# Twelve weight rests per hybrid attention loop: from VectorE's queue to GpSimd's

## The reference, cut to what matters

```python
def hybrid_mixer(h, w_in, b_in, w_out, sinks, group_gain, rel_bias):
    proj = h @ w_in + b_in
    qa, ka, va, qb, kb, vb = jnp.split(proj, IN_SPLITS, axis=-1)
    ...
    ya = swa_attention(qa, ka, va, sinks, rel_bias[:, :SWA_Q_HEADS])   # 8 heads, window of 128, a sink
    yb = moba_attention(qb, kb, vb, rel_bias[:, SWA_Q_HEADS:])         # 8 heads, causal on 256 tokens
    y = jnp.concatenate([rmsnorm(ya, group_gain[:SWA_WIDTH]),
                         rmsnorm(yb, group_gain[SWA_WIDTH:])], axis=-1)
    return y @ w_out
```

## Time and profile before

| | |
|---|---|
| median of 3 runs | 3169.53 us (3164.65 to 3184.48) |
| the profiled execution | 3166.69 us |
| its span in the trace | 3164.9 us |
| TensorE busy in the span | 97% |
| VectorE busy | 72% |
| ScalarE busy | 52% |
| GpSimd busy | 22% |
| granted TensorE clock | 0.99 |

### The profile page before, as it was taken

One profiled execution on the slowest core, in us unless ns is written; L12 is line 12 of the kernel. 1 busy time (PEld: TensorE's weight loads), 2 busy tenths in 40 slices (PEclk: granted clock), 3 DMA queues, 4 the chain that ended last, 5 costly groups with the idle time before them and its releaser, 6 DMA issues.

```text
span 3164.9 us, 58205 instructions
## 1 busy us (share of the span) xinstructions
PE 3075.8 (97%) x19824; PEld 2738.9 (87%) x19824; DVE 2264.8 (72%) x4160; ACT 1633.4 (52%) x3082; POOL 707.7 (22%) x704
## 2 busy tenths in 40 slices
PE   6999999999999999999999999999999999999999
PEld 5789999988888876799999888879988998988897
DVE  5649988877777535698788677777766777776754
ACT  1224568864444354354888544445446545445543
POOL 0107845520000110186455100001101010010000
PEclk9999999999999998999999999999999999999999
DMA  7644555558887430355443688777865687884454
GB/s 281 240 140 162 184 165 176 163 200 259 262 263 256 137 130 27 127 180 173 145 138 134 225 264 261 260 244 266 261 220 174 224 261 268 278 275 136 145 183 149
DMA packets 178000, 635.86 MB, mean 201 GB/s; under 512 B 23976, under 2 KB 23984, under 8 KB 177232
## 3 DMA queue, kind: packets, MB, share of 16 engines
q1 hardware_dynamic: 134560, 491.48, 46.6%
q0 software_dynamic: 43296, 142.77, 13.6%
q10 hardware_dynamic: 16, 0.01, 0.0%
HBM read 630.88 MB, written 9.53 MB: 202 GB/s over the span
## 4 chain that ended last, share of the span: by engine, by line
PE 90%; DVE 4%; DMA 2%; ACT 2%; DVEq 1%; issue 1%; SPq 0%; ACTq 0%; POOL 0%
PE ps L778 22%; PE ps L598 13%; PE ps L600 13%; PE ps L599 12%; PE ps L760 7%; PE ps L586 7%; PE ps L633 2%; PE ps L1172 2%; PE ps L1171 2%; PE ps L973 1%; DMA ring<-stream 1%; PE ps L1040 1%; PE ps L878 1%; PE ps L706 1%; DMA arena<-ada 1%
## 5 line engine op out<-in xcount | busy, mean ns | idle before, releaser
L1777 DVE TENSOR_TENSOR unit_low<-ring,unit_high 128x1024 fp32r<-128x1024 f32 x480 | 638.9, 1331 | 170.4 <-ACT unit_high L1272 162.0
L1272 ACT CAST unit_high<-ring 128x1024 fp32r<-128x1024 f32 x524 | 548.0, 1046 | 224.4 <-PE ps L600 166.9
L600 PE MATMUL ps<-expert_x_high,unit_low 128*128 128x256 f32 x1968 | 558.7, 284 | 0.0
L598 PE MATMUL ps<-expert_x_high,unit_high 128*128 128x256 f32 x1552 | 448.2, 289 | 1.9 <-DVE unit_low L1777 1.8
L599 PE MATMUL ps<-expert_x_low,unit_high 128*128 128x256 f32 x1552 | 435.1, 280 | 0.0
L600 PEld LDWEIGHTS ps<-expert_x_high,unit_low 128*128 128x128 f32 x1968 | 372.2, 189 | 0.0
L778 PE MATMUL ps<-unit_low,expert_high 128*128 128x512 f32 x1016 | 325.2, 402 | 1.8 <-DVE unit_low L1777 1.8
L778 PE MATMUL ps<-unit_high,expert_high 128*128 128x512 f32 x1016 | 318.0, 394 | 4.4 <-ACT unit_high L1272 4.4
L778 PE MATMUL ps<-unit_high,expert_low 128*128 128x512 f32 x1016 | 320.3, 396 | 0.1
L598 PEld LDWEIGHTS ps<-expert_x_high,unit_high 128*128 128x128 f32 x1552 | 295.0, 190 | 6.2 <-issue 2.4
L599 PEld LDWEIGHTS ps<-expert_x_low,unit_high 128*128 128x128 f32 x1552 | 293.6, 189 | 0.0
(11 more groups left out here) (393 smaller groups left out, 7027.4 us busy)
## 6 DMA issues: line engine op xcount, KB each, us to landing
ring<-stream SPq DMA_DIRECT2D x754, 512.0 KB, 4.0
arena<-stream SPq DMA_DIRECT2D x160, 512.0 KB, 4.3
score<-ada POOLq DMA_DIRECT2D x128, 512.0 KB, 5.0
arena<-ada POOLq DMA_DIRECT2D x96, 512.0 KB, 5.2
arena<-bias_tiles POOLq DMA_DIRECT2D x48, 192.0 KB, 2.7
arena<-ada SPq DMA_DIRECT2D x8, 1024.0 KB, 17.2
bias_tiles<-bias_rows POOLq DMA_DIRECT2D x8, 768.0 KB, 15.0
arena<-gate_home POOLq DMA_DIRECT2D x7, 512.0 KB, 9.9
```

Source lines behind the costliest of these rows:

```text
L598: pe.matmul(out, hi[:, kt, :], xh[:, kt, :], start=(kt == 0), stop=False)
L600: mm = pe.matmul(out, lo[:, kt, :], xh[:, kt, :], start=False, stop=(kt == KD - 1))
L1272: nc.scalar.copy(hi, raw_of(unit)).then_inc(whi_ready, 1)
L1777: V.tensor_tensor(out=lo, in0=raw_of(unit), in1=hi, op=ALU.subtract).then_inc(wlo_ready, 1)
```

## The change

In the attention loop of both hybrid mixers GpSimd makes the rests and VectorE makes none of them. By the code these are three in each of the four rounds, twelve for each mixer. VectorE keeps the three ahead of the loop and the five behind it, with two new waits that hand over the count: GpSimd waits for `wlo_ready` at n+2 before its first rest, and VectorE waits for n+3 before its next one. GpSimd's order in a round becomes: the first and second rest of the round, the two bias tiles of the next round's window half, the third rest, the two bias tiles of the next round's causal half, and then the additions of squares. The bias tiles of the first round are loaded ahead of it all.

```diff
--- before.py
+++ after.py
@@ VectorE, hyb @@
                     for k in range(2):
                         lowest(g, k, window[k])
-                    low(b + 2, m + 2)
                     for k in range(2):
                         normalize(g, k, window[k])
...
                         project(qs[:, 0], ps[1], b3[:, i + 1, :], -SCALE)
-                    if i == 3:
-                        low(b + 3, m + 3)
                     take_outputs(r, i)
...
                         lowest(g, k, causal[k])
-                    if i < 3:
-                        low(b + 4, m + 3)
                     for k in range(2):
                         normalize(g, k, causal[k])
-                    low(b + 5 if i < 3 else b + 4, m + 4)
                     take_outputs(r + 1, i + 4)
                 gained_low(6)
                 gained_low(7)
                 u, n = u + 14, n + 11
+                dve.wait_ge(wlo_ready, n + 3)
                 low(u + 3, n + 3)
@@ GpSimd, hyb @@
+                def biases(i, e):
+
+                    pool.wait_ge(o_read, i * 2 + (e + pair0[ph] - 1))
+                    for f in range(2):
+                        bias(e, f, i + (16 + 4 * f) if e == 0 else i * 2 + (24 + f))
+
+                u, n = start[ph] + 4, split0[ph] + 1
+                biases(0, 0)
+                biases(0, 1)
+                pool.wait_ge(wlo_ready, n + 2)
                 for i in range(4):
-                    for e in range(2):
-                        pool.wait_ge(o_read, i * 2 + (e + pair0[ph] - 1))
-                        for f in range(2):
-                            bias(e, f, i + (16 + 4 * f) if e == 0 else i * 2 + (24 + f))
+                    b, m = u + 4 * i, n + 3 * i
+                    low(b + 2, m + 2)
+                    low(b + 4 if i < 3 else b + 3, m + 3)
+                    if i < 3:
+                        biases(i + 1, 0)
+                    low(b + 5 if i < 3 else b + 4, m + 4)
+                    if i < 3:
+                        biases(i + 1, 1)
                     for r in (2 * i - 2, 2 * i - 1) if i >= 2 else ():
                         add_squares(r)
```

## The result

The changed kernel takes 3190.34 us (median of 17 runs, 3181.94 to 3198.18), the kernel before 3166.46 us (17 runs, 3156.3 to 3184.48). The ratio is 1.0076 with a 95% interval of 1.0066 to 1.0087, so the change costs 24 us. The profiled execution has a span of 3188.4 us, against 3164.9 us.

The account below looks back on a forecast made before the run. TensorE was taken to bound the loops, tight against VectorE's path through normalize and `project`. Terms 13.5 + 1.8 + 4.6 - 0.5 = 19.4 us gave 3189 us against the median; the 8-in-10 range was 3171 to 3205.

Parts of the forecast that it names:

- What bounds it: Attention loops: TensorE bounds, tight against VectorE's path to `project` with 0.34 us of margin; any gain at most 5.3 us.
- The 0.5 us taken for the last round: Last round: removing VectorE's rest between `project` and `take_outputs` gains 0.24 us per mixer, 0.5 us together.
- The first rests start without waiting for the transfers: Each round's first GpSimd rest follows the bias issue, not its transfer; third round: ends 2399.30, 1.7 us of cover.
- Rival 2: GpSimd's queue bounds: rests wait for transfers, or the additions' drain delays the last three; +28 to +45 us, chance 0.15.
- The exclusion of rests and normalizes: Loops: a GpSimd rest and VectorE's `normalize` (L2013, L2023) share a port pair; whichever issues second waits a whole instruction.
- Rounds 2 and 3: Window halves: rests catch both heads' normalizes, delaying `project`; TensorE stands 3.2 us three times and 3.9 us once, 13.5 us.
- Causal halves: Rounds one to three: the third rest holds both normalizes' scalings, second head's transposes 0.3 us late six times, 1.8 us.
- Last round: Three rests behind two additions of squares; the third holds the second causal head's scaling 2.3 us per mixer, 4.6 us.
- My upper bound: Last round: additions were once 4.34 us behind their issue instead of 3.14; a slip there moves all three rests.

Follow-up runs that it names:

- `dummy_tt`: Kernel before, VectorE making all rests, plus twelve GpSimd subtractions per mixer at the change's places that nobody waits for; ratio 1.0076 to before.
- `project_first`: Changed kernel with the `project` that empties ps1 put ahead of the window pair's normalizes on VectorE; ratio 1.0038 to the kernel before.
- `fill_short`: Changed kernel with 18 unread matmuls (2.1 us) on TensorE ahead of its wait for `project` in rounds two and three; loops 180.9 against 187.1 us.
- `squares_last`: Changed kernel with all additions of squares behind the last round's rests instead of two ahead of them; loops 185.4 against 187.1 us, single execution.
- `dummy_set`: Kernel before, plus GpSimd memsets at the change's places that nobody waits for; loops 168.5 against 160.5 us, single execution.

## Why the prediction was right

The forecast was 3189 us, by +19.4; the change measured +24 us, its loops +26.5. By the steps of the prediction:

- **What bounds it** was right: the 0.34 us between `project` and the third product group was the first thing lost, and VectorE's 29 us of relief bought nothing that shows. The 0.5 us taken for the last round can't be seen in any row.
- **The first rest starts without waiting for the transfers**, right: the issue ends at 2400.51 and the rest starts at 2400.53. Rival 2's waits did not come in rounds 2 and 3.
- **The exclusion of rests and normalizes**, right, and shown from both sides: by `dummy_tt` (no rest moved, VectorE held, as much lost in all) and by `project_first` (the same rests, a hold of 3.92 us, 18.0 of the 18.4 us of rounds 2 and 3 gone).
- **Rounds 2 and 3**: the term of 13.5 us measured 18.4. Its waits were over-sized, at 10.3 us: 3.70 for the 3.9 forecast, but 2.1 to 2.2 for 3.2, since the second head's sink addition and reciprocal slipped through before the second rest, and only its scaling was caught. The 3.9 was met by luck: I had one head slip between the two rests and the second caught, while in the trace the first head's L2013 was held through both rests and nothing was held after it. What was missing is the term that I put at nothing, TensorE's time behind a wait, 8.1 us; by `fill_short` 7.1 of it are the granted clock. I had read the clock of 1.00 in the loop and never asked what it would be after a wait of 2 to 4 us.
- **Causal halves**: 1.8 us forecast, 0 measured (7.94 us before and after). The first head's scaling is held (2.20 us), but VectorE's own rest no longer stands ahead of it, and both heads are ready in time.
- **Last round**: 4.6 us forecast, 8.1 measured, and most of it by another mechanism. I let the third rest catch the second head's scaling and took the late first and second rests as covered. The additions of squares ahead of them were the late part (idle 4.50 and 7.20 us where I had taken 3.14), and TensorE waited for the rests themselves (1.05 and 0.68 us in hyb0, 3.62 in hyb1), which is rival 2 in this place; behind the 3.62 us the clock took 1.2 us more. The hold of the normalizes, my 2.3 us per mixer, was 1.3 us in hyb0, and in hyb1 TensorE did not wait for it. My upper bound named it; my value did not.

- **Rival 2's upper end** was summed wrongly: its own terms, 10 us for four rounds and 8 us for two last rounds on top of 19.4, give +37, not +45.

For the loops the forecast was 7.1 us short: 8.1 us left out behind the waits, 3.5 too few in the last round and 0.5 of gain that did not come, against 3.2 too many in the waits and 1.8 too many in the causal halves. That the total came as near as it did is in part luck, since these errors offset each other. The sign and the cause held, and of the rivals only a part of rival 2 was seen. The mark that I gave for it, "TensorE waits on L2613 itself", is met in the last round.

## What to carry to other kernels

Before work goes from VectorE to GpSimd, list what VectorE runs at those moments, down to instructions on two elements, and who waits behind them: the cost was not GpSimd's 2.4 us but whom it held. If TensorE waits behind the held engine, add what its clock loses after the wait. Reordering the held engine, so that what TensorE needs first comes first, gave back 17 of the 26.5 us; the other 9 us needed the last round's rests back on VectorE.

## What the runs showed of the hardware

- A waiting VectorE instruction was passed over by a second GpSimd instruction: L2013 was held 4.72 us, through two rests of 2.4 us each, when it came just as the first began. In round 3 it was held for one, 1.20 us.
- The hold is not a matter of size: instructions on 2 elements per partition lasted 1.61 us (L2260, 0.17 alone) and 4.72 us (L2013, 0.15 alone). Beside a fill, which reads nothing, L2013's like kept its 0.15 us.
- The minimum instructions (L2004, PSUM with one SBUF input) and `project` kept their lengths beside rests in all kernels (0.28 to 0.35 us and 0.42 to 0.49 us for the two sizes of the minimum, 0.47 to 0.49 us for `project`).
- TensorE idle for 3.70 us ran the next 5.3 us at half clock and lost 2.6 us by it; with idle times of 2.1 to 2.2 us it lost 1.5 us. With 2.2 us of filler in the same wait, and 1.7 us idle, it lost nothing.
- The length of the wait alone does not settle it. Behind waits of 2.1 to 2.2 us the granted clock fell to 0.50 in eight of ten cases (not behind 2.13 us in `squares_last` and 2.23 us in `dummy_set`), behind 2.4 to 2.6 us in one of four (`dummy_tt`), and behind 3.70 us in all three, where round 2 took 18.29, 18.03 and 17.27 us. What decides between these cases, no run here tells.
